# Weight slots: the low part over the raw data, and the split two slots ahead

## The reference

```
p = h @ w_in                                   # 2048 -> q, k, v, gates, low-rank parts
layers 0, 1: y = [grouped-query attention * silu(g_gqa), latent attention * silu(g_mla)]
             latent: q = rms(cq) @ w_uq, k and v = rms(ckv) @ w_ukv
layers 2, 3: y = [multi-scale pooling, mixed by a 256x256 matrix per group, * silu,
                  differential attention * silu]
x = x + gate * (y @ w_out)
```

## Time and profile before

| | |
|---|---|
| median of three runs | 3244.1 us (3240.6 to 3244.69) |
| profiled execution | 3241.01 us, its span 3239.1 us |
| TensorE busy (matmul / weight load) | 93% / 73% |
| VectorE / ScalarE / GpSimd busy | 50% / 32% / 3% |
| mean granted TensorE clock | 0.967 |
| HBM traffic | 152 GB/s over the span |
| weight slots | 500 of 512 KB, median 3.5 us from issue to landing |
| ada units | 192 of 1 MB |

### The profile page before, as it was taken

The page is one execution under the profiler, slowest core; times in us unless marked ns, Lnnn a source line. Parts: engine busy times, 40 slices in busy tenths (PEclk is TensorE's granted clock), DMA queues, the critical chain, the costliest instruction groups (busy, mean ns, idle before and its releaser), DMA issues. The chain is left out here.

```text
span 3239.1 us, 40895 instructions
## 1 busy us (share of the span) xinstructions
PE 3027.7 (93%) x17158; PEld 2362.8 (73%) x17158; DVE 1605.7 (50%) x2493; ACT 1023.4 (32%) x1508; POOL 102.0 (3%) x157
## 2 busy tenths in 40 slices
PE   5899999999997999999878999999999979999988
PEld 1577777785675787886766779766776758798888
DVE  2334333355435554454556373555473455747574
ACT  2212233223312332332323221334342123315453
POOL 0000000000000000000000000240000000003100
PEclk7899999999998999999989999999999989999999
DMA  8644433221543643741763444333445433222455
GB/s 321 274 169 143 144 130 130 98 73 45 183 174 137 227 176 121 268 132 65 272 225 126 154 151 166 132 111 111 150 158 206 163 116 117 85 92 92 137 169 169
DMA packets 120135, 495.10 MB, mean 153 GB/s; under 512 B 11792, under 2 KB 30480, under 8 KB 95120
## 3 DMA queue, kind: packets, MB, share of 16 engines
q1 hardware_dynamic: 99648, 463.51, 40.2%
q10 hardware_dynamic: 20304, 28.97, 2.6%
HBM read 484.05 MB, written 8.39 MB: 152 GB/s over the span
## 5 line engine op out<-in xcount | busy, mean ns | idle before, releaser
L1294 PE MATMUL products<-h_high,w_high 128*128 128x512 f32 (+1 forms) x3424 | 1256.2, 367 | 91.4 <-DVE h_low L932 47.1
L1294 PE MATMUL products<-h_low,w_high 128*128 128x512 f32 (+1 forms) x3424 | 1189.7, 347 | 0.0
L1294 PE MATMUL products<-h_high,w_low 128*128 128x512 f32 (+1 forms) x3424 | 1189.2, 347 | 0.0
L849 DVE TENSOR_TENSOR w_low<-w_raw,w_high 128x1024 fp32r<-128x1024 f32 x500 | 615.3, 1231 | 819.6 <-ACT w_high L547 817.1
L547 ACT CAST w_high<-w_raw 128x1024 fp32r<-128x1024 f32 x500 | 522.9, 1046 | 1382.4 <-PE products L1294 1333.8
L1294 PEld LDWEIGHTS products<-h_high,w_high 128*128 128x128 f32 x3424 | 657.3, 192 | 341.9 <-issue 228.0
L1294 PEld LDWEIGHTS products<-h_low,w_high 128*128 128x128 f32 x3424 | 659.0, 192 | 81.0 <-issue 13.0
L1294 PEld LDWEIGHTS products<-h_high,w_low 128*128 128x128 f32 x3424 | 657.4, 192 | 81.6
L1294 PE MATMUL products<-w_high,h_high 128*128 128x256 f32 x640 | 184.1, 288 | 0.5 <-issue 0.5
L1294 PE MATMUL products<-w_high,h_low 128*128 128x256 f32 x640 | 181.1, 283 | 0.0
L1294 PE MATMUL products<-w_low,h_high 128*128 128x256 f32 x640 | 181.0, 283 | 0.0
(11 more groups left out here) (193 smaller groups left out, 2676.9 us busy)
## 6 DMA issues: line engine op xcount, KB each, us to landing
w_raw<-w_slots SPq DMA_DIRECT2D x500, 512.0 KB, 3.5
ada_w<-ada_slots SPq DMA_DIRECT2D x174, 1024.0 KB, 6.0
mix_b<-ada_slots SPq DMA_DIRECT2D x18, 1024.0 KB, 9.8
x_residual<-x ACTq DMA_DIRECT2D x2, 4096.0 KB, 23.0
x_scratch<-x_residual ACTq DMA_DIRECT2D x3, 2048.0 KB, 8.0
x_residual<-x_scratch ACTq DMA_DIRECT2D x3, 2048.0 KB, 9.2
x_residual<-ctx ACTq DMA_DIRECT2D x2, 2048.0 KB, 16.2
out<-x_residual ACTq DMA_DIRECT2D x1, 2048.0 KB, 7.8
```

The source lines that it names most:

```text
L849: nc.vector.tensor_tensor(wlo[:, n % SPL, :], raw[:, n % RAW, :], whi[:, n % SPL, :].bitcast(F32), ALU.subtract).then_inc(low_done, 1)
L1294: ins = nc.tensor.matmul(o, a, b, start=first and q == 0, stop=last and q == 2, skip_group_check=skip)
```

## The change

`w_low` gets five slots and takes the memory of `w_raw`: the subtraction writes over the raw slot that it reads. `w_raw` has five slots instead of four, `w_high` three instead of two; both kernels hold eight slots in all. ScalarE and VectorE split slot n+2 where they split n+1: in the rounds, in `short`, `kr` and `mix`, with one split fewer among the chunks of `apply` and `ysplit`. The phase before does one more. For the slots of a mix phase, whose raw data must stay, both engines do a one-column copy in place of the split. SyncE's code is unchanged save for RAW. TensorE's and GpSimd's are unchanged too, but for the slots' numbers in the ring.

```diff
--- before.py
+++ after.py
@@ -25,8 +25,9 @@
 
 
 SLOT = 1024
-RAW = 4
-SPL = 2
+RAW = 5
+HIGH = 3
+LOOK = 2
 KS = 4
 GF = 256
 ADA_UNIT = 2048
@@ -248,8 +249,8 @@
         Q = place("mix_a", [P, HEADS, T])
         G = place("mix_b", [P, HEADS, T])
         raw = place("w_raw", [P, RAW, SLOT])
-        whi = place("w_high", [P, SPL, SLOT], F32R)
-        wlo = place("w_low", [P, SPL, SLOT], F32R)
+        wlo = place("w_low", [P, RAW, SLOT], F32R, at=cursor[0] - 4 * RAW * SLOT)
+        whi = place("w_high", [P, HIGH, SLOT], F32R)
         ada_base = cursor[0]
         ada_w = place("ada_w", [P, 2, ADA_UNIT])
         ckh = place("c_kv_high", [P, RC, T], F32R, at=ada_base)
@@ -358,6 +359,7 @@
                     FREE.append((freed_dve, nd))
 
 
+        MIX_SLOTS = {ph["at"]["slot"] + k for ph in PH if ph["kind"] == "mix" for k in range(2)}
         HEAD_AT, KNORMS, GROUP_FREED, HEADS_DONE, KROOTS_DONE, FD_AT = {}, [0], [], {}, {}, {}
         for ph in PH:
             FD_AT[ph["at"]["slot"]] = ph["at"]["fd"]
@@ -402,7 +404,7 @@
 
         def split_beside(pi, t, split):
 
-            beside = {5: {3: 1, 5: 2, 7: 3, 10: 4, 13: 5}, 3: {3: 1, 7: 2, 11: 3}}[PH[pi + 1]["ahead"]]
+            beside = {5: {3: 2, 5: 3, 7: 4, 10: 5}, 3: {3: 2, 7: 3}}[PH[pi + 1]["ahead"]]
             if t in beside:
                 split(PH[pi + 1]["at"]["slot"] + beside[t])
 
@@ -542,9 +544,13 @@
 
                 act.wait_ge(raw_landed[n % RAW], 16 * (n // RAW + 1))
 
-                if n >= SPL:
-                    act.wait_ge(slot_used, n - SPL + 1)
-                nc.scalar.copy(whi[:, n % SPL, :], raw[:, n % RAW, :]).then_inc(high_done, 1)
+                if n >= HIGH:
+                    act.wait_ge(slot_used, n - HIGH + 1)
+                if n in MIX_SLOTS:
+
+                    nc.scalar.copy(whi[:, n % HIGH, 0:1], raw[:, n % RAW, 0:1]).then_inc(high_done, 1)
+                    return
+                nc.scalar.copy(whi[:, n % HIGH, :], raw[:, n % RAW, :]).then_inc(high_done, 1)
 
             def row_copy(b, units):
 
@@ -630,6 +636,7 @@
                             evac(0, 0)
                         high(k)
                 high(8)
+                high(9)
                 evac(0, 1)
 
             def head_side(ph, k):
@@ -771,8 +778,8 @@
                             opening(evac)
                             return
                         for k in range(8):
-                            if 8 * i + k >= ph["ahead"]:
-                                high(n0 + 8 * i + k + 1)
+                            if 8 * i + k + LOOK > ph["ahead"]:
+                                high(n0 + 8 * i + k + LOOK)
                             if k == evac_slot(ph, i):
                                 evac(i, 0)
                             head_side(ph, 8 * i + k)
@@ -787,7 +794,7 @@
                     rounds(ph, round_)
                 elif kind in ("short", "kr", "mix"):
                     for k in range(len(ph["evac"]) if kind == "short" else 2):
-                        high(at["slot"] + k + 1)
+                        high(at["slot"] + k + LOOK)
                         att_side(ph, at["slot"] + k)
                         rank_side(ph, k)
                 elif kind == "attn":
@@ -846,7 +853,11 @@
                     return
 
                 dve.wait_ge(high_done, n + 1)
-                nc.vector.tensor_tensor(wlo[:, n % SPL, :], raw[:, n % RAW, :], whi[:, n % SPL, :].bitcast(F32),
+                if n in MIX_SLOTS:
+
+                    nc.vector.tensor_copy(whi[:, n % HIGH, 0:1], raw[:, n % RAW, 0:1]).then_inc(low_done, 1)
+                    return
+                nc.vector.tensor_tensor(wlo[:, n % RAW, :], raw[:, n % RAW, :], whi[:, n % HIGH, :].bitcast(F32),
                                         ALU.subtract).then_inc(low_done, 1)
 
             def ada_columns(b):
@@ -953,6 +964,7 @@
                             evac(0, 0)
                         low(k)
                 low(8)
+                low(9)
                 evac(0, 1)
 
             def head_side(ph, k):
@@ -1203,8 +1215,8 @@
                             opening(evac)
                             return
                         for k in range(8):
-                            if 8 * i + k >= ph["ahead"]:
-                                low(n0 + 8 * i + k + 1)
+                            if 8 * i + k + LOOK > ph["ahead"]:
+                                low(n0 + 8 * i + k + LOOK)
                             if k == evac_slot(ph, i):
                                 evac(i, 0)
                             head_side(ph, 8 * i + k)
@@ -1224,7 +1236,7 @@
                     toks, layer = ph["toks"], ph["layer"]
                     n = toks.stop - toks.start
                     for k, (name, g, mode) in enumerate(ph["evac"]):
-                        low(at["slot"] + k + 1)
+                        low(at["slot"] + k + LOOK)
                         rank_side(ph, k)
                         if 1 <= k <= len(ph["turn"]):
 
@@ -1313,8 +1325,8 @@
 
             def feature_chunk(n, half, kk, ks, rhs_h, rhs_l, w, first, last, tiles=2):
 
-                wh = whi[:, n % SPL, :].rearrange("p (k f) -> p k f", k=ks)
-                wl = wlo[:, n % SPL, :].rearrange("p (k f) -> p k f", k=ks)
+                wh = whi[:, n % HIGH, :].rearrange("p (k f) -> p k f", k=ks)
+                wl = wlo[:, n % RAW, :].rearrange("p (k f) -> p k f", k=ks)
                 for t in range(tiles):
                     f = slice(t * P, (t + 1) * P)
                     ins = three(M[:, 2 * half + t, 0:w], [(wh[:, kk, f], rhs_h), (wh[:, kk, f], rhs_l),
@@ -1324,8 +1336,8 @@
             def token_chunk(n, half, kk, xh, xl, first, last):
 
 
-                wh = whi[:, n % SPL, :].rearrange("p (k f) -> p k f", k=KS)
-                wl = wlo[:, n % SPL, :].rearrange("p (k f) -> p k f", k=KS)
+                wh = whi[:, n % HIGH, :].rearrange("p (k f) -> p k f", k=KS)
+                wl = wlo[:, n % RAW, :].rearrange("p (k f) -> p k f", k=KS)
                 for t in range(4):
                     tk = slice(t * P, (t + 1) * P)
                     o = M[:, 2 * half + t // 2, (t % 2) * GF:(t % 2 + 1) * GF]
```

## The result

The changed kernel takes 3257.86 us (median of 6 runs, 3254.29 to 3258.79) against 3244.11 for the kernel before on the same chip: a ratio of 1.0042, 95% interval 1.0029 to 1.0055, so 13.75 us slower, between 9 and 18. The prediction was 3250.7 us with a range of 3238 to 3262 and its largest chance, 0.45, on slower. Sign and range hold. The size doesn't: +6.6 was forecast, and a little over twice that came.

The account below looks back on a forecast made before the run. TensorE, busy 93% of the span, was taken as the bound. Losses of 16.8 + 2.0 + 0.15 less gains of 12.3 gave +6.6 us on the median of 3244.1: 3250.7 us, range 3238 to 3262.

Parts of the forecast that it names:

- What stays: Steady-run copies and subtractions keep their moments and order; subtracting over the raw slot takes equally long: 0 us.
- w_low waits: TensorE's waits for w_low: 3.3 us off in out of layer 1, 2.0 k, 1.0 attn_g, 1.2 short cq, 0.3 others.
- The normalisation: Apply stretches have one split fewer: layer 3 gains 2.2 us, layers 0 and 2 nothing, layer 1 loses 0.15.
- The mix slots: One-column copies take two subtractions from ahead of the eviction in layer 3's mix: 2.3 us gained; layer 2, 0.
- The hole: Ahead of latent attention in layers 0 and 1, engines wait for out's late second slot: 8.5 plus 8.3, 16.8 us lost.
- The clock after the hole: First attention steps after each hole run at TensorE's lower clock: 1.0 us each, 2.0 lost; bounds 0 and 3 per hole.
- Rival 3: Landings cost more than the hole: ScalarE blocked in layer 1's ada rounds delays evictions and softmax; +18.6, 3262.7 us; chance 0.15.
- Rival 1: The lead pays for the hole, all w_low waits going: -9.4, 3234.7 us; hole absent, 3232; together chance 0.13.
- Rival 2: Gains and holes cancel, or the following ysplit hides part of the hole: +0 to +5, 3244 to 3249 us; chance 0.37.
- The forecast's own band: Whole-kernel time around the forecast sum, 3249 to 3257 us; chance 0.35.

Follow-up runs that it names:

- gate_one_ahead: slot_first with layer 3's attn_g split one slot ahead, all else two ahead: 3232.67 us, ratio 0.9972 to the kernel before.
- slot_first: Changed kernel, but SyncE issues out's second weight slot (layers 0, 1) ahead of its wait and the modulation unit: 3234.51 us, ratio 0.9971 to the kernel before.
- before_wait: Kernel before, with ScalarE and VectorE waiting at the end of short ckv for out's second slot to land, no longer lead: 3262.85 us, ratio 1.0067.

## Why the prediction was half right

Term by term, in the prediction's order.

- *What stays: 0.* Right. The subtraction over the raw slot takes as long as the old one.
- *w_low waits.* k of layer 3: 2.0 forecast, 1.8 found. attn_g: 1.0, and 0.9. short cq: 1.2, and 1.2. Out of layer 1: 3.3 forecast, 1.8 to 2.4 found: the three stalls went and the one at the late transfer stayed, as said, but each is worth some 0.8 us with its restart, where 1.1 had been put down from the mean of all waits.
- *The normalisation.* Layer 3: 2.2, and 2.4. Layer 1: 0.15 lost was forecast and 1.0 to 1.2 won; the late transfer of its fourth slot did hold up ScalarE (the shift rose by 2.9 us there), but the next two slots gave back more.
- *The mix slots: 2.3 forecast, nothing found.* The first term that failed. The step "two of them come ahead of the eviction on which GpSimd waits" is right as to their place, but "2 x 1.15" took VectorE to be the only engine on that path: ScalarE took 1.0 back, and the lower clock behind it 1.7, more than the 0.9 that had arrived.
- *Not in the sum:* out of layer 3 is 0.7 us later. TensorE's wait for h_low ahead of its first product is 5.2 us in place of 4.6; gate_one_ahead, with a lead of one there, doesn't have it.
- *The hole: 16.8 forecast, 16.5 found.* Its parts were right to 0.3 us.
- *The clock after the hole: 2.0 forecast, 6.9 and 7.4 found.* The second term that failed, and the larger one. The prediction took "1.0 each, since the first steps are mostly VectorE and ScalarE". At half clock TensorE itself is the bound of these steps (19.89 of 20 us busy), and the level doesn't come back after 3 us but after 14. The upper bound that was given, 3 us a hole, was too low as well by both medians, though within their error; it rested on a stretch of 3 us of products, and the attention isn't such a stretch. The Trainium skill's page "TensorE: Matmul & The Clock Gate" (section "What's actually happening") puts this ramp under 1% of a typical kernel's span and advises against fitting a model to a count of slow matmuls; that it be left out altogether is the prediction's reading of it. 7 us is 0.2% of this span, so the sentence holds here; but it is half of what the change cost, and a term of 0 would have been the larger error.

The sum: 16.5 + 6.9 - 8.6 = 14.8 us on the medians of the shared runs, against 16.8 + 2.0 + 0.15 - 12.3 = 6.6. The clock makes 4.9 of the 8.2 between them, and the gains, 3.7 smaller, most of the rest. Of these 3.7, the mix slots are 2.3 and out of layer 1 about 1.

Of the rivals Rival 3 came nearest in time (3262.7), for the wrong reason: ScalarE's waits for landings grew to 256.6 us, but slot_first keeps 218.0 of them and is the faster kernel. They are hidden. Rival 1 was right in one point: with the hole absent the kernel is faster; its 3232 for that case compares with 3234.5 measured. Rival 2, with 0 to 5 us, is out: the interval begins at 9. The forecast's own band, 3249 to 3257, was missed by 0.9 us. That the range holds is partly luck: its upper end, 3262, was Rival 3's sum, and what Rival 3 describes didn't happen.

## What to carry to other kernels

When work is moved ahead, list what is queued in front of its input as well as what stands behind the work itself: here one wait, put there for another transfer's sake, held up a slot that nobody had wanted so early, and three engines with it. Moving that slot ahead of the wait turned +0.4% into -0.3%. Price a pause of TensorE at more than its length, and by the work that follows it: here two pauses of 6 to 8 us were followed by 14 to 19 us of attention at the lower clock, some 3.5 us of loss each by the medians, while the products of layer 3's apply were back at the upper level after 3.8 us. Which work stays low for long has to be looked up in a trace in which it starts low.

## What the runs showed that was not expected

- A hole of 8.2 us is followed by 14.1 us (layer 0) and 16.5 us (layer 1) of scores at a granted clock of 0.50, and one of 6.2 us by 19.4 us (layer 0 of before_wait; 16.0 in its layer 1). Without a hole, gate_one_ahead has 13.7 us at 0.50 in layer 1, beginning 1.7 us behind the start of the scores. Eight matmuls that fill 7.03 of the 9.84 us change the stretch behind the holes by 0.3 us or less and the time by nothing that could be measured.
- Kernels without a hole have 3.4 to 10.2 us at 0.50 in the first latent attention, worth up to 2.7 us: as much as most terms of this case. Stage by stage comparisons of two single executions must be read with that in mind.
- One execution of the filled kernel took 4548.56 us at a mean granted clock of 0.62; its other ten were between 3250 and 3262. Nothing here says why.
- A lead of one with three high slots was worth 3.8 us (0.6 to 6.5): in attn_g of layer 3 ScalarE had been late for the squares because its copies waited for a high slot.
